# Expert down weights laid row-major per partition, hidden columns taken in pairs, and w_in's first block loaded ahead of the early modulation section

## The reference

```python
sh1, sc1, gt1, sh2, sc2, gt2 = split(silu(cond) @ w_mod[l] + b_mod[l], 6)     # modulation, 6 x 1024
h = rmsnorm(x, g_mix[l]) * (1 + sc1) + sh1
aq, ak, av, mq, mk, mv, mo, mi, mf = split(h @ w_in[l])                      # 1024 -> 2832 columns
att, h_ml = attention(aq, ak, av), bidirectional_mlstm(mq, mk, mv, mi, mf)
x = x + gt1 * (concat(att, sigmoid(mo) * norm(h_ml)) @ w_out[l])
h = rmsnorm(x, g_ffn[l]) * (1 + sc2) + sh2
# 16 experts of width 512, each token goes to two of them
hid = silu(h @ w_e_gate[l, e]) * (h @ w_e_up[l, e]) * gate                   # 1024 -> 512
x = x + gt2 * sum_e(hid @ w_e_down[l, e])                                    # 512 -> 1024
```

## Time and profile before

| | |
|---|---|
| three plain runs | 813.96, 815.18, 817.14 us |
| the profiled execution | 814.25 us, of it 812.5 us from the first to the last instruction |
| TensorE matmul | 770.4 us busy (95%) |
| TensorE weight load | 476.6 us busy |
| VectorE | 263.0 us busy (32%) |
| ScalarE | 159.9 us busy (20%) |
| GpSimd | 54.3 us busy (7%) |
| SyncE's DMA queue | 285.30 MB, 53712 packets, 87.3% of 16 engines' span |

### The profile page before, as it was taken

One profiled execution on the slowest core, in us unless ns is written; L12 is line 12 of the kernel. 1 busy time (PEld: TensorE's weight loads), 2 busy tenths in 40 slices (PEclk: granted clock), 3 DMA queues, 4 the chain that ended last, 5 costly groups with the idle time before them and its releaser, 6 DMA issues.

```text
span 812.5 us, 13029 instructions
## 1 busy us (share of the span) xinstructions
PE 770.4 (95%) x5759; PEld 476.6 (59%) x5763; DVE 263.0 (32%) x509; ACT 159.9 (20%) x352; POOL 54.3 (7%) x65
## 2 busy tenths in 40 slices
PE   4799999999999999999979999999999999999997
PEld 2265646785655665555523746688665565555653
DVE  0203185525412233122231303882343233213223
ACT  3210115403211110110021111261241201102001
POOL 0040060100100000000000002400010000000000
PEclk9999999999999999999999999999999999999999
DMA  8998459999999999999999964318959999999994
GB/s 353 387 356 348 181 199 404 387 420 361 389 425 418 416 429 419 415 428 420 404 409 397 388 238 168 150 55 335 424 211 415 419 420 427 415 418 427 418 410 153
DMA packets 55498, 289.56 MB, mean 356 GB/s; under 512 B 3400, under 2 KB 5760, under 8 KB 42128
## 3 DMA queue, kind: packets, MB, share of 16 engines
q1 hardware_dynamic: 53712, 285.30, 87.3%
q0 software_dynamic: 1488, 3.31, 1.3%
q10 hardware_dynamic: 240, 0.08, 0.0%
HBM read 286.31 MB, written 2.37 MB: 355 GB/s over the span
## 4 chain that ended last, share of the span: by engine, by line
PE 78%; DMA 9%; SPq 7%; DVE 4%; issue 2%; POOL 1%; ACT 0%; DVEq 0%
PE ps L1071 23%; PE ps L734 14%; PE ps L1097 11%; PE ps L988 7%; DMA ring<-in_w_in 6%; SPq L577 5%; PE ps L1056 4%; PE ps L628 4%; PE ps L746 3%; DMA ring<-in_w_e_down 2%; PE ps L1111 2%; SPq L573 1%; PE ps L864 1%; PE ps L1082 1%; PE ps L889 1%
## 5 line engine op out<-in xcount | busy, mean ns | idle before, releaser
L1071 PE MATMUL ps<-ring,xe 128*64 128x256 f32 x1376 | 152.4, 380 | 3.5 <-DMA ring<-in_w_e_up 3.5
L1071 PEld LDWEIGHTS ps<-ring,xe 128*64 128x64 f32 x1376 | 98.4, 137 | 59.8 <-issue 9.6
L734 PE MATMUL ps<-ring,hT 128*128 128x512 f32 (+1 forms) x320 | 128.5, 562 | 4.8 <-DMA ring<-in_w_in 4.8
L734 PEld LDWEIGHTS ps<-ring,hT 128*128 128x128 f32 x320 | 61.6, 194 | 69.1 <-issue 60.3
L1097 PE MATMUL ps<-ring,ex 128*32 128x512 f32 x736 | 92.4, 594 | 2.4 <-DMA ring<-in_w_e_down 1.6
L1910 DVE COPY ye<-ps 64x512 f32<-64x512 f32 (+1 forms) x28 | 19.3, 689 | 165.5 <-PE ps L1097 165.4
L1097 PEld LDWEIGHTS ps<-ring,ex 128*32 128x32 f32 x736 | 26.8, 110 | 53.9 <-issue 52.8
L988 PE MATMUL ps<-hT,ring 128*128 128x256 f32 x256 | 57.1, 381 | 0.0
L1894 DVE RECIPROCAL ex<-ex 128x512 f32<-128x512 f32 x16 | 53.6, 3353 | 0.6
L988 PEld LDWEIGHTS ps<-hT,ring 128*128 128x128 f32 x256 | 48.0, 190 | 7.2 <-issue 0.8
L628 PE MATMUL ps<-ring,cT 128*32 128x512 f32 (+1 forms) x448 | 46.1, 536 | 3.5 <-DMA ring<-in_w_mod 3.1
(11 more groups left out here) (263 smaller groups left out, 747.4 us busy)
## 6 DMA issues: line engine op xcount, KB each, us to landing
ring<-in_w_mod SPq DMA_DIRECT2D x24, 2048.0 KB, 12.7
ring<-in_w_e_up SPq DMA_DIRECT2D x23, 2048.0 KB, 19.6
ring<-in_w_e_gate SPq DMA_DIRECT2D x20, 2048.0 KB, 21.8
ring<-in_w_e_down SPq DMA_DIRECT2D x19, 2048.0 KB, 22.4
ring<-in_w_in SPq DMA_DIRECT2D x10, 2048.0 KB, 23.8
beside<-in_w_e_gate SPq DMA_DIRECT2D x8, 2048.0 KB, 20.9
beside<-in_w_e_down SPq DMA_DIRECT2D x7, 2048.0 KB, 20.0
beside<-in_w_e_up SPq DMA_DIRECT2D x5, 2048.0 KB, 18.1
```

Of the source, the lines that this page charges most:

```text
L734: mm = pe.matmul(bank[:, 0:width], hT[:, k, b * P:(b + 1) * P], w[:, k, :], start=(k == 0), stop=(k == KD - 1))
L1071: mm = pe.matmul(bank[64 * h:64 * h + 64, 256 * j:256 * j + 256], xe[:, k, c:c + PLACES], w[:, k, 256 * h:256 * h + 256], start=(k == 0), ...
```

## The change

Three edits. First, `w_down` is read as `(p k) n`: partition p holds rows 4p to 4p+3, one run of 16 KB. The products must then have hidden column 4p+k on partition p, which is made in two steps: the gate and up products take as moving operand, for half h, the columns 4q+2h and 4q+2h+1 for q = 0 to 127 (two floats, then two left out) in place of 256 columns in a row, and each transpose takes every second column of `hid`. Second, the last pair's down blocks are halved by rows (two runs joined to 8 KB a partition) and `down(7)` makes both output halves from the first two k, then both from the last two. Third, at the start of layer 1 `mk` is loaded first, then the four blocks of the early section, and on TensorE the section's four row products stand together behind both halves of the `mk` product. The path for more than 32 tokens of an expert is adapted too; it isn't entered here.

```diff
--- before.py
+++ after.py
@@ -246,12 +246,9 @@
     for i in range(section_slots(0, 0)):
         put(("mod", 0, 0, i))
     for l in range(DEPTH):
-        for sec in early_sections(l):
-            for i in (0, 1):
-                put(("mod", *sec, i))
         put(("mk", l))
         for sec in early_sections(l):
-            for i in (2, 3):
+            for i in range(section_slots(*sec)):
                 put(("mod", *sec, i))
         for g in list(PROJ)[1:]:
             put((g, l))
@@ -493,7 +490,7 @@
             w_out = t["w_out"].rearrange("l (k p) n -> l p k n", p=P)
             w_gate = t["w_e_gate"].rearrange("l e (p k) n -> l e p k n", p=P)
             w_up = t["w_e_up"].rearrange("l e (p k) n -> l e p k n", p=P)
-            w_down = t["w_e_down"].rearrange("l e (k p) n -> l e p k n", p=P)
+            w_down = t["w_e_down"].rearrange("l e (p k) n -> l e p k n", p=P)
 
             def expert_read(l, p, i):
 
@@ -543,13 +540,11 @@
                 sp.dma_start(xtok[:, b, :], t[name][0]).then_inc(x_in, 16)
             load_section(0, 0, 1, 2, 3)
             for l in range(DEPTH):
-                for sec in early_sections(l):
-                    load_section(*sec, 0, 1)
                 for g, (c0, width) in PROJ.items():
                     load((g, l), w_in[l, :, :, c0:c0 + width], width)
                     if g == "mk":
                         for sec in early_sections(l):
-                            load_section(*sec, 2, 3)
+                            load_section(*sec)
                 for sec in later_sections(l)[:-1]:
                     load_section(*sec)
                 for i in range(2):
@@ -569,13 +564,13 @@
                             elif slot == OVER:
                                 full(sp, (("mlT", 1), l))
                                 sp.wait_ge(state_out, 16 * STATE_OUTS * (l + 1))
-                        width = D // parts if i >= 4 else KD * WB // k
-                        sp.dma_start(slot_space(slot).rearrange("p (k n) -> p k n", k=k)[:, :, 0:width],
-                                     w[l, 2 * p + j, :, :, 0:width]).then_inc(slot_landed[slot], 16)
+                        n = k // parts if i >= 4 else k
+                        sp.dma_start(slot_space(slot).rearrange("p (k n) -> p k n", k=k)[:, 0:n, :],
+                                     w[l, 2 * p + j, :, 0:n, :]).then_inc(slot_landed[slot], 16)
                 for j in range(2):
                     slot = weights["expert", l, PAIRS - 1, 4 + j][0]
-                    sp.dma_start(slot_space(slot).rearrange("p (k n) -> p k n", k=KF)[:, :, D // 2:D],
-                                 w_down[l, 2 * PAIRS - 2 + j, :, :, D // 2:D]).then_inc(last_half, 16)
+                    sp.dma_start(slot_space(slot).rearrange("p (k n) -> p k n", k=KF)[:, KF // 2:KF, :],
+                                 w_down[l, 2 * PAIRS - 2 + j, :, KF // 2:KF, :]).then_inc(last_half, 16)
                 with sp.If(largest(sp, l) > SLOTS):
                     for p in range(PAIRS - 2, PAIRS):
                         for i in range(6):
@@ -708,16 +703,12 @@
                 done(("x", r), mm)
 
             for l in range(DEPTH):
-                for sec in early_sections(l):
-                    section_rows(*sec, 0)
                 if l == 0:
                     pe.wait_ge(cond_silu, 1)
                     section_rows(0, 0, 0)
                 for i in range(4):
                     norm_parts(l, i)
                 norm_total(l)
-                for sec in early_sections(l):
-                    section_rows(*sec, 1)
                 if l == 0:
                     section_rows(0, 0, 1, 2, 3)
                     section_columns(0, 0)
@@ -793,11 +784,9 @@
                                     done(key, mm)
 
                 project("mk", (0,), fresh=True)
-                for sec in early_sections(l):
-                    section_rows(*sec, 2)
                 project("mk", (1,), fresh=True)
                 for sec in early_sections(l):
-                    section_rows(*sec, 3)
+                    section_rows(*sec, 0, 1, 2, 3)
                     section_columns(*sec)
                 gates()
                 project_turned("mq", (0,))
@@ -1069,7 +1058,7 @@
                                 taken(pe, (("gather", p // 2, k // 2), l))
                             for h in range(2):
                                 mm = pe.matmul(bank[64 * h:64 * h + 64, 256 * j:256 * j + 256], xe[:, k, c:c + PLACES],
-                                               w[:, k, 256 * h:256 * h + 256], start=(k == 0), stop=(k == KD - 1))
+                                               w[:, k, :].rearrange("p (q c) -> p q c", c=KF)[:, :, 2 * h:2 * h + 2], start=(k == 0), stop=(k == KD - 1))
                         if j == 0:
                             mm.then_inc(first_read, 1)
                     done(key, mm)
@@ -1078,25 +1067,30 @@
 
                     taken(pe, (("up", p), l))
                     bank = begin((("turn", p), l))
+                    pairs = hid[:, :, :].rearrange("p k q -> p (k q)").rearrange("p (j q c) -> p j c q", j=2, c=2)
                     for k in range(KF):
-                        mm = pe.transpose(bank[:, k * P:(k + 1) * P], hid[:, k, :], ident)
+                        mm = pe.transpose(bank[:, k * P:(k + 1) * P], pairs[:, k // 2, k % 2, :], ident)
                     done((("turn", p), l), mm)
 
                 def down(p):
 
                     w = [landed(("expert", l, p, 4 + j)).rearrange("p (k n) -> p k n", k=KF) for j in range(2)]
                     taken(pe, (("turn", p), l))
-                    for half in range(2):
-                        bank = begin((("down", p, half), l))
-                        if p == PAIRS - 1 and half == 1:
+                    for part in range(2 if p == PAIRS - 1 else 1):
+                        ks = range(2 * part, 2 * part + 2) if p == PAIRS - 1 else range(KF)
+                        if part == 1:
                             pe.wait_ge(last_half, 32 * (l + 1))
-                        for k in range(KF):
-                            for g in range(4):
-                                j, b = g % 2, (g // 2 + turned(p)) % 2
-                                c = k // 2 * PLACES + b * SLOTS
-                                mm = pe.matmul(bank[32 * g:32 * g + 32, :], hidT[:, 2 * j + k % 2, c:c + SLOTS],
-                                               w[j][:, k, half * 512:(half + 1) * 512], start=(k == 0), stop=(k == KF - 1))
-                        done((("down", p, half), l), mm)
+                        for half in range(2):
+                            key = (("down", p, half), l)
+                            bank = begin(key) if part == 0 else ps[banks[key][0]]
+                            for k in ks:
+                                for g in range(4):
+                                    j, b = g % 2, (g // 2 + turned(p)) % 2
+                                    c = k // 2 * PLACES + b * SLOTS
+                                    mm = pe.matmul(bank[32 * g:32 * g + 32, :], hidT[:, 2 * j + k % 2, c:c + SLOTS],
+                                                   w[j][:, k, half * 512:(half + 1) * 512], start=(k == 0), stop=(k == KF - 1))
+                            if ks[-1] == KF - 1:
+                                done(key, mm)
 
                 def sums(b, dj):
...
```

More of the change, by code:

```diff
@@ L1940, in spill @@
                     dve.wait_ge(spill_silu[l], m + 5)
-                    dve.tensor_tensor(hid[0:PLACES, :, :].rearrange("p k q -> p (k q)"), ps[3][0:PLACES, :], some,
-                                      ALU.mult).then_inc(spill_act[l], 1)
+                    dve.tensor_tensor(hid[0:PLACES, :, :].rearrange("p k q -> p q k"), ps[3][0:PLACES, :].rearrange("p (q k) -> p q k", k=KF),
+                                      some.rearrange("p (q k) -> p q k", k=KF), ALU.mult).then_inc(spill_act[l], 1)
                     dve.wait_ge(spill_turned[l], n)
```

## The result

Ten runs of each kernel were timed: the changed one has a median of 819.73 us (818.03 to 820.86), the kernel before 816.15 us (813.96 to 819.69). The ratio is 1.0043 with a 95% interval of 1.0026 to 1.0059, so the change made the kernel about 3.5 us slower. The profiled execution took 819.73 us, 817.9 of it from the first to the last instruction, 5.4 us more than before's 812.5; before's profiled execution (814.25 us) was 1.9 us under its own median, which is most of the difference between 3.5 and 5.4.

What follows compares the result with a forecast made beforehand. TensorE's chain in the experts and the DMA of weights were taken as limits side by side; -3.1 (layer 0) + 1.2 (order) - 3.0 (layer 1) = -4.9 us gave 810.2 us against the median, range 806.5 to 817.

Steps and rivals of the forecast that it cites:

- Part 2: Strided operands of gate and up products and transpositions: no cost, zero; bounds 223 us for products, 7 us for transpositions.
- Rival (a): Gate and up products (L1071): strided stream slower than contiguous, 223 us times the slowing share; chance 0.13.
- turning point (4%): Slowing of the strided gate and up products from which the kernel would be over 0.5% (4.1 us) slower.
- The prediction's sign for this: Gate and up instructions (L1071): a mean above 390 ns would show the forecast wrong; 380 ns was expected.
- Part 1: Longer `w_down` runs in the experts: weights arrive earlier, 3.1 us gained in layer 0 and 3.0 in layer 1.
- It just suffices: Last pairs: 2.2 us gained ahead of up blocks, 2.2 needed; 3.1 ahead of last halves, 3.3 or 3.1 needed.
- Part 4: Start of layer 1, `mk` first: order costs 3.7 us, gives 2.6 back, net 1.2 slower; 35.3 us to the gates.
- rival (c): Start of layer 1: emptier norm costs clock, norm and `mk` products slower, one or two times 1.7 us; chance 0.15.
- the sum: Whole kernel: -3.1 (layer 0) + 1.2 (order) - 3.0 (layer 1) = -4.9 us.
- Part 3: Last pair's down products, halves by rows: wait stays in the middle, first output half's copy is covered; zero.

Runs made afterwards that it cites:

- undo_order: The changed kernel with the old order of `mk` and the section's row products put back; median 813.88 us, ratio 0.9979 to the kernel before.
- runs_only: The kernel before with only the 16 KB runs of `w_down` and the last pair's halves by rows; 807.98 us, ratio 0.9902.
- pairs_only: The kernel before with only the gate and up products reading two floats and leaving two out; 816.18 us, ratio 1.0021.
- runs8_whole: undo_order with `w_down` in two 8 KB runs a partition and contiguous gate and up products; 809.97 us, ratio 0.9930 to the kernel before.
- order_only: The kernel before with only the new order, `mk` loaded first and four row products behind its product; median 818.63 us, ratio 1.0046.

## Why the prediction was wrong

Forecast: 810.2 us, 0.6% faster; measured 819.73, 0.4% slower, outside the range. By its steps:

**Part 2, the step that failed.** "I take zero, since a float32 column streams at half the engine's rate already." The measured price is 0.69 us a pair for the products and 0.04 for the transpositions, 11.7 us of work in all, 4.9% on L1071. The reasoning had the right two quantities and no number for one of them: it counted on two columns' time (1.70 ns) being enough to read past a gap, and the runs show 1.79 ns for it. Rival (a) named this mechanism, its place and its turning point (4%), and had a chance of 0.13. By the work it adds, 4.9% is just beyond that point. But part of that work took the place of waits: the kernel with the runs and the stride and without the order was still 0.2% faster (undo_order), and it took the order as well to make it slower. The prediction's sign for this, a mean of an L1071 instruction above 390 ns, was set too far off: the mean was 388. An instruction lasts 380 ns in the trace but the next one of its half follows after 218, so the mean grew by 2% where the products' time grew by 4.9%.

**What the 11.7 us became.** undo_order against runs_only is the stride on top of the longer runs: (0.9979 - 0.9902) x 816 = 6.3 us, give or take 3 by the two intervals. The other 5.4 us must be waits that a slower TensorE no longer has; the traces show 4.2 of them, 2.3 us for up blocks, 0.7 under "issue" ahead of down products and 1.2 ahead of `mk`. Read one after the other, the ratios say: longer runs alone -8.0 us, strided reads +6.3, order +5.2. That they add up to +3.5 is no check, since each is a difference to the kernel before it in this row.

**Part 1, the runs.** The mechanism was right and the size about right: 6.1 us forecast for the experts and 2.6 for `mk`, and runs_only shows 5.0 and 3.0 in its trace, 8.0 us by the ratio. The rate over the experts of layer 1 rose from 421 to 427 GB/s; pairs_only, with 4 KB runs and the stride, has 421. "It just suffices" was not so: without the stride 2.3 us of waits for up blocks stayed. The list of waits was short by pair 6's, 1.64 and 0.77 us, which the table of waits calls "issue"; this did not change the sign.

**Part 4, the order.** Forecast for the stage 35.3 us, measured 35.9. The two row products on the path were right. Mis-sized was the clock: one slow half of `mk` (8.83 us) was carried over, and 15.91 us for both halves bear that out, but the emptier norm ran slow as well, which is rival (c): `mk` starts 427.39 - 415.75 = 11.6 us behind the last scatter, where 422.2 - 411.6 = 10.6 were forecast (the rest of the stage came 0.4 us shorter than forecast). A second point doesn't touch the sum, in which the 2.6 us of the `mk` wait stand once: they were put down to the order, though part 1 by itself brings `mk` nearly in time. Beside part 1 the order had only its price, two row products and the clock, 5.2 us, and not 1.2.

**Part 3, the halves.** No DMA wait in the middle of down(7), and the first output half's copy is covered: as forecast, but for what the end of the kernel shows, below.

**Left open.** In the kernels with the new `down` (the changed one, undo_order, runs_only, runs8_whole) TensorE stands 1.6 to 2.0 us under "issue" ahead of its last transpositions (L1223 here), and the last stage is up to 0.6 us longer; before, order_only and pairs_only don't have it. What TensorE waits for there no view names, and it wasn't tried. The wait itself delays nothing: in before, after, runs_only and undo_order alike the last transposition ends 6.1 us and the last output is issued 6.9 us behind the start of the last scatter. What grows is the time from that issue to the end, 2.5 us in before, where the four outputs are issued over 3.2 us, and 3.0 us after, where they are issued over 1.5. Also not tried were the halves by rows without 16 KB runs, and what two floats of one line with a gap between them cost.

## What to carry to other kernels

A stride that is called free is free only up to a rate: work out how many 16-byte lines (or jumps) the stream wants in a nanosecond, and measure one product with it before it stands on the path of a whole kernel. When an engine and the DMA are nearly level, price edits in pairs: a slower engine hides DMA waits, a faster DMA makes a reordering needless, and the same microseconds must not be counted for both. Before you move filler work out of an engine's gaps, look at the granted clock of the work behind them.

## What the runs showed of the hardware

A float32 moving operand that was read with a stride got one 16-byte line, or one jump of the address, in 1.78 to 1.79 ns for each stream, with two streams side by side and, at two floats a line, with four; columns go at 0.85 ns. Reading two floats of each line cost 4.9% (14.65 against 13.96 us), one float 109% (29.14 us), four of each eight nothing (13.96). Four transpositions whose stationary operand takes every second float took 0.47 to 0.48 us instead of 0.44. Loads in runs of 16, 4 and 2 KB a partition moved at 429, 410 and 385 GB/s in stretches of 13, 4 and 4 us.
